# A hybrid conformer, mLSTM and mixture-of-experts block on one core: the last sigmoid products laid among the recurrence, SiLU rests and key products moved, one output-projection tile pair split into two passes, bias vectors loaded earlier

## The reference, cut to what matters

```python
u = rms_norm(h, norm_mix_g[l]);  z = u @ w_in[l] + b_in[l]          # h: 16 meta tokens + 512 tokens, 1024 wide
conv_out  = conformer_conv(z[..., GLU_OFF:Q_OFF], ...)              # GLU, 31-tap conv, layer norm, silu, pointwise matmul
mlstm_out = mlstm_branch(z, mlstm_norm_g[l], mlstm_out_w[l])        # recurrence, norm of each head, sigmoid gate, matmul
g_conv, g_mlstm = sigmoid(z[..., GC_OFF:GM_OFF]), sigmoid(z[..., GM_OFF:N_IN])
h = h + (g_conv * conv_out + g_mlstm * mlstm_out) @ w_out[l]
h = h + moe_ffn(rms_norm(h, norm_ffn_g[l]), ...)                    # 32 experts, top 4
out = rms_norm(h, final_norm_g)
```

## Time and profile before

| | us |
|---|---|
| median of 3 runs | 1623.09 (1620.73 to 1624.62) |
| time of the profiled execution | 1621.82 |
| its span | 1620.0 |
| PE busy | 1580.6 (98%) |
| GpSimd busy | 427.9 (26%) |
| DVE busy | 651.3 (40%) |
| ACT busy | 395.8 (24%) |
| chain that ended last: PE / DMA | 82% / 8% |

### The profile page before, as it was taken

How to read it: one execution, slowest core, us unless ns; L and a number is a source line. 1 busy time by engine, 2 the same in 40 slices (tenths; PEclk the granted TensorE clock), 3 DMA queues, 4 the chain that set the end, 5 groups by cost and what they waited for, 6 DMA issues and landing times.

```text
span 1620.0 us, 38897 instructions
## 1 busy us (share of the span) xinstructions
PE 1580.6 (98%) x16450; PEld 925.2 (57%) x16450; DVE 651.3 (40%) x1245; ACT 395.8 (24%) x605; POOL 427.9 (26%) x465
## 2 busy tenths in 40 slices
PE   6999999998999899999999999999999999999997
PEld 6998988876889634444444444334433444444444
DVE  4799898026241624222422242224222422242247
ACT  5333134255221511111111111111111111111112
POOL 7334334371433621211121112111211121112114
PEclk9999999999999899999999999999999999999999
DMA  7553243320275289999999999999999999999995
GB/s 215 157 182 105 79 144 90 105 78 27 78 298 212 84 300 411 408 409 414 413 408 403 410 411 406 406 409 410 399 409 406 411 395 402 407 411 400 400 416 243
DMA packets 132436, 492.91 MB, mean 304 GB/s; under 512 B 17305, under 2 KB 74817, under 8 KB 82628
## 3 DMA queue, kind: packets, MB, share of 16 engines
q1 hardware_dynamic: 114020, 464.98, 73.2%
q0 software_dynamic: 8736, 16.22, 3.1%
q10 hardware_dynamic: 9632, 11.03, 2.2%
HBM read 476.32 MB, written 24.87 MB: 309 GB/s over the span
## 4 chain that ended last, share of the span: by engine, by line
PE 82%; DMA 8%; POOL 2%; ACT 2%; DVE 2%; SPq 2%; issue 1%; POOLq 0%; DVEq 0%; ACTq 0%
PE banks L1532 36%; PE banks L1104 25%; PE banks L1581 17%; DMA w_ring<-in_expert_w_dram 7%; PE banks L1519 1%; POOL slot_table L693 1%; DVE mix_lo L1898 1%; SPq L442 1%; DMA small<-in_b_in_dram 0%; POOL h_res L759 0%; ACT banks L991 0%; ACT w_hi L800 0%; PE banks L1552 0%; ACT conv L954 0%; SPq L524 0%
## 5 line engine op out<-in xcount | busy, mean ns | idle before, releaser
L1532 PE MATMUL banks<-w_ring,xT 128*32 128x512 f32 x6144 | 671.5, 592 | 4.9 <-DMA w_ring<-in_expert_w_dram 4.0
L1532 PEld LDWEIGHTS banks<-w_ring,xT 128*32 128x32 f32 x6144 | 206.9, 110 | 429.9 <-issue 423.6
L1581 PE MATMUL banks<-w_ring,actT 128*32 128x256 f32 x6144 | 344.6, 380 | 0.0
L1581 PEld LDWEIGHTS banks<-w_ring,actT 128*32 128x32 f32 x6144 | 205.7, 110 | 134.3 <-issue 18.0
L2011 DVE TENSOR_TENSOR hid<-banks,bias 128x512 f32<-128x512 f32 x96 | 63.9, 665 | 477.4 <-PE banks L1532 477.4
L633 POOL TENSOR_TENSOR w_lo<-stage,w_hi 128x2048 fp32r<-128x2048 f32 x38 | 175.2, 4611 | 264.1 <-ACT w_hi L800 264.1
L1104 PE MATMUL banks<-u_hi,w_hi 128*128 128x264 f32 (+1 forms) x528 | 175.6, 333 | 0.3 <-ACT gates L914 0.3
L1104 PE MATMUL banks<-u_hi,w_lo 128*128 128x264 f32 (+1 forms) x528 | 174.6, 331 | 0.0
L1104 PE MATMUL banks<-u_lo,w_hi 128*128 128x264 f32 (+1 forms) x528 | 174.2, 330 | 0.0
L703 POOL COPY token_now<-token_of 96x1 int32 (+1 forms) x33 | 6.1, 183 | 568.7 <-PE banks L1519 564.9
L1065 ACT ACTIVATE bias<-banks 128x512 f32<-128x512 f32 x32 | 19.1, 597 | 560.5 <-PE banks L1552 560.5
(11 more groups left out here) (298 smaller groups left out, 1626.8 us busy)
## 6 DMA issues: line engine op xcount, KB each, us to landing
w_ring<-in_expert_w_dram SPq DMA_DIRECT2D x384, 1024.0 KB, 22.5
stage<-in_w_in_dram SPq DMA_DIRECT2D x20, 1024.0 KB, 5.3
stage<-in_w_in_dram SPq DMA_DIRECT2D x16, 512.0 KB, 5.3
y_rows<-empty_row ACTq DMA_DIRECT2D x8, 1024.0 KB, 4.7
y_in<-y_rows SPq DMA_DIRECT2D x4, 2048.0 KB, 22.4
stage<-in_conv_pw_w_dram SPq DMA_DIRECT2D x4, 1024.0 KB, 5.1
stage<-in_mlstm_out_w_dram SPq DMA_DIRECT2D x4, 1024.0 KB, 5.1
stage<-in_w_out_dram SPq DMA_DIRECT2D x4, 1024.0 KB, 5.5
```

The lines of the kernel that those rows point to most:

```text
L1532: last = nc.tensor.matmul(banks[32 * g:32 * (g + 1), t].rearrange("p (c j) -> p c j", j=64), xT[:, k, 32 * t:32 * (t + 1)], units, start=k ...
L1581: last = nc.tensor.matmul(banks[32 * g:32 * (g + 1), 3 + t, 0:GRP], actT[:, t, k], w2_ring[k // 2][:, k % 2, GRP * g:GRP * (g + 1)], start ...
```

## The change

Six edits in one. (1) The four tiles of the last sigmoid pair are taken apart (`last_sigmoid`): two stand before the meta-token state products, the third before the state products of chunk 1, the fourth behind the numerators of tile 0, with two state products and the key transposes of chunk 2 inside it after its fifth k-step. The third and fourth go into bank 0, not banks 4 and 5. (2) The squares go to a bf16 scratch in SBUF (`head_squares`, over `mean_w`) and not to PSUM, and the numerators of the next tile wait on `h_taken`, not on `h_squared`. (3) The key transposes of chunk 3 stand inside the numerators of tile 2; `pointwise(0, 0)` is cut in two, its first tile ahead of the hidden transposes of tile 2. (4) On DVE `silu_rests(0)` leaves its place before tile 0 and stands with `silu_rests(1)` behind tile 1; on ACT the order of sigmoids, splits, keys and `silu_highs` follows; on GpSimd the second half of the PW weights is split behind the root of tile 0. (5) WO pair 0, half s=1: for token tiles 0 and 1 the products with `w_hi` run first, behind a wait for `w_hi` alone, and those with `w_lo` after `wait_weights`. (6) The second half of the first GLU pair is loaded behind the twelve vector transfers.

```diff
@@ sync
-            load_glu(0, first=True)
+            load_glu(0, (0,), first=True)
...
+            load_glu(0, (1,), first=True)
             sp.dma_start(vb_bc, b_in[:, V_OFF:V_OFF + D].to_broadcast([P, D])).then_inc(row_bc_in, 16)
@@ gpsimd
-            split_pair(PW_PAIR)
+            split_pair(PW_PAIR, (0,))
 
             for i in range(TT):
                 pool.wait_ge(h_squared, HEADS * (i + 1))
                 rstd(P, head_square, head_rstd, DV)
                 nc.gpsimd.tensor_tensor(head_scale, head_rstd, den_inv, ALU.mult).then_inc(h_scaled, 1)
+                if i == 0:
+                    split_pair(PW_PAIR, (1,))
@@ scalar
+            def head_sums(i):
+
                 act.wait_ge(h_taken, i + 1)
                 for h in range(HEADS):
-                    nc.scalar.activation(banks[:, 4 + h, 0:DV], h_buf[i % 2][:, h], ACT.Square, scale=den_inv[:, h:h + 1],
+                    if i or h >= 2:
+                        act.wait_ge(h_squared, HEADS * i + h - 1)
+                    nc.scalar.activation(head_squares[:, h % 2], h_buf[i % 2][:, h], ACT.Square, scale=den_inv[:, h:h + 1],
                                          accum_out=head_square[:, h:h + 1]).then_inc(h_squared, 1)
...
+            def last_sigmoid(t):
+
+                act.wait_ge(mm_done, pair_tick(SIG_PAIR + 5, LAST_TICKS[t]))
+                nc.scalar.activation(gates[:, 3 * KT - 4 + t], banks[:, LAST_BANKS[t]], ACT.Sigmoid,
+                                     bias=vec[:, B_SIG + 3 * KT - 4 + t:B_SIG + 3 * KT - 3 + t]).then_inc(sig_out, 1)
+
+            scaled_keys(0)
+            last_sigmoid(0)
+            last_sigmoid(1)
+            split_hi(PW_PAIR, 0)
+            scaled_keys(1)
+            last_sigmoid(2)
+            head_sums(0)
+            scaled_heads(0)
+            scaled_keys(2)
+            last_sigmoid(3)
+            split_hi(PW_PAIR, 1)
+            silu_highs(0)
+            for i in range(1, TT):
+                if i == 2:
+                    scaled_keys(3)
+                head_sums(i)
+                silu_highs(i)
+                scaled_heads(i)
+                split_hidden(i - 1)
             split_hidden(TT - 1)
@@ tensor
-            sigmoid_tiles(5)
...
+            def numerators(i):
+
                 pe.wait_ge(head_out, HEADS + 1)
-                pe.wait_ge(h_squared, HEADS * i)
+                if i:
+
+                    pe.wait_ge(h_taken, i)
                 for h in range(HEADS):
                     nc.tensor.matmul(banks[:, 4 + h, 0:VW], probs[:, h, P * i:P * (i + 1)], v_sb[:, i, h], start=True, stop=False)
                     pe.wait_ge(state_out, HEADS * i + h + 1)
                     nc.tensor.matmul(banks[:, 4 + h, 0:VW], q_sb[:, h, P * i:P * (i + 1)], state[:, h],
                                      start=False, stop=True).then_inc(h_mm, 1)
+                    if i == 2 and h == 2:
+                        key_transposes(3)
+
+            def rest_of_state():
+                state_part(1, (2, 3))
+                key_transposes(2)
+
+            wait_weights(SIG_PAIR + 5, 0)
+            pe.wait_ge(sig_out, 3 * KT - 5)
+            last_sigmoid(0)
+            pe.wait_ge(sig_out, 3 * KT - 4)
+            last_sigmoid(1)
+            state_part(0)
+            key_transposes(1)
+            wait_weights(SIG_PAIR + 5, 1)
+
+            pe.wait_ge(normed, KT)
+            last_sigmoid(2)
+            state_part(1, (0, 1))
+
+            pe.wait_ge(sig_out, 3 * KT - 2)
+            numerators(0)
+            pe.wait_ge(sig_out, 3 * KT - 1)
+            last_sigmoid(3, rest_of_state)
+            for i in range(1, TT):
+                numerators(i)
+                if i + 1 < TT:
                     hidden_transposes(i - 1, (0,))
                     state_part(i + 1, (0, 1))
                     hidden_transposes(i - 1, (1,))
                     state_part(i + 1, (2, 3))
                 else:
-                    hidden_transposes(i - 1)
-
                     pe.wait_ge(state_out, HEADS * TT)
                     pe.wait_ge(silu_lo_made, KT)
-                    pointwise(0, 0)
+                    pointwise(0, 0, (0,))
+                    hidden_transposes(i - 1)
+                    pointwise(0, 0, (1,))
             hidden_transposes(TT - 1)
...
+                    if j == 0:
+                        pe.wait_ge(w_hi_made[1], WO_PAIR + 1)
+                        for low in range(2):
+                            if low:
+                                wait_weights(WO_PAIR, 1)
+                            for i in range(2):
+                                span = slice(P * i, P * (i + 1))
+                                for k in range(KT):
+                                    terms = ((mix_hi, w_lo),) if low else ((mix_hi, w_hi), (mix_lo, w_hi))
...
+                    for i in range(0 if j else 2, TT):
@@ vector
             update_state(0)
-            silu_rests(0)
             for i in range(TT):
...
+                if i == 1:
+                    silu_rests(0)
+                    silu_rests(1)
+                elif i == 2:
+                    silu_rests(2)
                 if i >= 2:
                     split_rest(i - 2)
-                if i:
-                    silu_rests(i)
```

More of the change, by code:

```diff
@@ L1338, in _, with pointwise @@
             whole = slice(0, SEQ)
-            def pointwise(j, s):
+            def pointwise(j, s, parts=range(GT)):
                 wait_weights(PW_PAIR + j, s)
-                for c in range(GT):
+                for c in parts:
                     if j:
@@ L1425, in _ @@
                         continue
-                    for i in range(TT):
+                    if j == 0:
[7 more added lines that the diff above has]
+                                    terms = ((mix_hi, w_lo),) if low else ((mix_hi, w_hi), (mix_lo, w_hi))
+                                    for m, (rows, w) in enumerate(terms):
+                                        last = nc.tensor.matmul(banks[:, 4 + i, GRP:2 * GRP], rows[:, k, span], w[:, 1, k],
+                                                                start=not low and k == 0 and m == 0, stop=low == 1 and k == KT - 1)
+                                if low:
+                                    last.then_inc(mm_done, 1)
+                    for i in range(0 if j else 2, TT):
                         token_tile(s, (mix_hi, mix_lo), banks[:, 4 * (1 - j) + i, GRP * s:GRP * (s + 1)],
```

44 lines of the change are left out of this document (16 added, 28 removed).

## The result

| | before | after |
|---|---|---|
| median | 1622.74 us (1620.73 to 1624.62, 4 runs) | 1609.63 us (1607.62 to 1610.73, 4 runs) |
| profiled execution | 1621.82 | 1610.73 |
| its span | 1620.0 | 1609.0 |

Two longer comparisons later gave the same program 0.9931 (0.9917 to 0.9946) and 0.9938 (0.9924 to 0.9951), 11.2 and 10.1 us; all 15 runs of it have a median of 1610.7. So some 2 to 3 us of the 13.1 were the draw of these runs, and 4 to 5 us are left for which the prediction must answer.

What follows compares the result with a forecast made beforehand. PE was taken to bound everything before the experts. Recurrence 4.0 (9.6 - 3.9 - 1.7), WO 1.9 and start 0.5 sum to 6.4 us: profiled 1621.8 becomes 1615.4, median 1.3 above, 1616.7 us; range 1612.3 to 1621.3.

Steps and rivals of the forecast that it cites:

- the 1.82: PE's hole at 24.5, waiting for the vectors: removed there but probably moved to the third GLU unit; 0.5 us taken as won.
- Its landing times: At the start, the second GLU half lands at 26.2 and is ready for PE at 33.0, wanted at 31.0.
- their terms: New PE holes in the recurrence: 0.7 for DVE's state, 2.0 for tok_made, 0.9 for chunk 3 keys, 0.3 for silu_lo; 3.9 us.
- I count one slow stretch: In the recurrence's new order, one half-clock stretch near the new hole at 377 costs 1.7 us; bounds none and two.
- both slow stretches lose their cause: Recurrence, 360 to 366 and 370 to 376: meta products between dense tiles and no hole at 367 remove causes of 3.4 us.
- rival C: Recurrence: DVE's rests meet GpSimd's w_lo, delaying DVE and tile 1's root 4 us; recurrence wins nothing, 1620.7 us; chance 0.20.
- WO: Output projection: PE's 1.90 us hole at 495.8 goes whole, 1.9 us won, at least 1.5 for an added handoff.
- D: Experts: their stream, at DMA share 1.01, starts by something other than PE, hiding the gain; 1623 us; chance 0.06.
- B: Recurrence and start: no slow stretch (1.7) and the vectors' 1.8 won whole, 3.0 us more, 1613.7 us; chance 0.20.
- the 1.8: At the start, the vectors' stall is won whole if small transfers hold the queue for less than 5.2 us.
- no slow stretch at all: Recurrence: between dense tiles the rows show no cause for a lower clock, so 1.7 us more is won.
- E: Start: second GLU half issued only after small transfers leave the queue; PE loses 8.0 us there, 1625.2 us; chance 0.04.

Runs made afterwards that it cites:

- the moved root: Changed kernel with the second half of the PW weights split behind the root of tile 1 on GpSimd, not ahead of it: 1614.99 us, ratio 0.9954.
- the PSUM run: Changed kernel with edit 2 undone, squares written back to PSUM and the next numerators waiting on them: one profile, 1610.43 us.
- the fills: Changed kernel with unread products before the third GLU unit and tile 1's hidden transposes: 1616.01 us oversized, with router fills too; 1617.74 us resized, without them.
- WO alone: Kernel before with only the output projection's edit (5): 1619.35 us, ratio 0.9988.
- vectors alone: Kernel before with only the new order of the first loads (edit 6): 1618.39 us, ratio 0.9985.
- the start filled: Kernel before with 16 unread products laid where PE waits for the vectors at 24.5: 1620.30 us against 1622.18, ratio 0.9988.
- The recurrence alone: Kernel before with only the edits of the recurrence (1 to 4): 1615.67 us, ratio 0.9966.

## Why the prediction was right and wrong

Since single profiles differ by the stretches, I take for each part the mean over the profiles whose order and holes are the same in that part (their count in brackets).

| stretch | old order | new order | won | forecast |
|---|---|---|---|---|
| start to key transposes | 336.6 (4) | 333.7 (7) | 3.0 | 0.5 |
| to `pointwise(0, 1)` | 70.6 (5) | 66.1 (5) | 4.5 | 4.0 |
| to the router, at full clock | 129.4 (4) | 127.2 (9) | 2.2 | 1.9 |
| router to the end | 1082.2 (5) | 1082.6 (5) | -0.4 | 0 |

Sum 9.2, where the runs say 10 to 11; the 1 to 2 us between stand in no row. (The second row leaves out the moved root, the PSUM run and the fills; the fourth takes, for the new order, the changed kernel's three profiles, the PSUM one and the moved root, and leaves out WO alone for the old, which would make the -0.4 a -0.3.)

**The start: wrong, and the step that failed is the price of the hole.** The prediction costed "the 1.82" as idle time and asked only whether it moves. Its landing times were right to 0.2 us. But the hole also brings a slow stretch behind it, 2.1 us in the mean of four profiles, and the moved hole doesn't; with 0.9 that the hole itself is shorter by (2.05 us at 24.5 in the mean of four profiles, 1.11 at 31 in the mean of seven), that makes 3.0 where I took 0.5. That is 2.5 of the 4 to 5 us that were to be explained. In the profile of before nothing showed it, since that execution happened to have none at 26; the same profile did show it at 360 and 370, and there I had priced it. I priced the clock where the one profile had it, and not where the same kind of hole stood without.

**The recurrence: right in the mean, for half of the reasons.** Each hole went where the rows said, and the new ones came within 0.3 us of their terms (0.7, 2.0, 0.9, 0.3 forecast; 0.66, 2.07, 0.63, 0.16 found). Wrong is the step "I count one slow stretch": the old order loses 2.05 us of work in the mean of five profiles, the new one 2.05 too (none twice, 3.4 three times). So "both slow stretches lose their cause" was wrong: with the meta products between dense tiles their stretch came in five of nine profiles, and behind the new hole at 377 there was one in five of seven. The change won nothing by the clock here.

Wrong too, though it didn't show in the sum, is that each stretch of the old order costs its 1.7. Where it lies on the first numerators (before in both profiles, and WO alone), the hole behind it is 2.20; where it comes only behind that hole (vectors alone, and the start filled), the hole is 3.90. Vectors alone:

```profile
367.61 1.72 PE L1336 MATMUL banks<-v_sb,kw_sb 128*128 128x257 f32 x4 [3.90 <-DVE state L1829]
```

PE stands there for DVE, which comes at the same time either way, so the slow numerators were covered by the wait. And DVE is late through its three rests, which in the profile of before (as in the other four) stand beside a `w_lo` until 365.02:

```profile
360.50 4.52 POOL L633 TENSOR_TENSOR w_lo<-stage,w_hi 128x2048 fp32r<-128x2048 f32 x1 [2.50 <-ACT w_hi L800]
```
```profile
362.55 4.22 DVE L1851 TENSOR_TENSOR silu_lo<-conv,silu_hi 128x512 fp32r<-128x512 f32 x3 [1.85 <-ACT silu_hi L982]
```

Three rests without `w_lo` take 1.89. So rival C's meeting already stood in the kernel before, under the name of DVE's state update, and edit 4 takes `silu_rests(0)` out of it; what that edit is worth alone no run shows.

At the full clock the old order would take 69.85 us (WO alone and the second profile of before, whose only stretch is a covered one), the new one takes 64.57: 5.3 won, 4.3 of it idle time. From this 0.8 goes off in the mean, because slow stretches make the new order 1.6 us longer and the old one, with one of its places covered, only 0.8. That gives the 4.5 of the table (in idle time 6.73 less 3.48, in busy time 63.90 less 62.66). Why the busy rows are 1.0 to 1.2 us shorter for the same matmuls I can't name. The first profile, with no slow stretch, shows 6.96; the 2.5 above the mean are luck in both profiles of that pair, before with one stretch that cost and after with none.

**WO: right.** 2.16 in every pair of profiles at full clock, against 1.9. The 0.3 more is not shown. The recurrence alone, which keeps this hole, had a slow stretch behind it once (494 to 500); the other four that keep it, none.

**The router: left out.** Its slow stretches lose 1.7 to 5.1 us of PE's work in all profiles without a fill. Leaving them out did no harm, because the chain to the second expert runs through GpSimd's slot table, SP and the weights, and not through them. Of the 1.5 us in the first table 1.3 are GpSimd's: from the router's first product until GpSimd was through with its last indirect transfer it was 32.27 us before and 31.01 after, but 31.00 in the second profile of before, and 31.27 with the moved root, whose router stage loses the same 5.1 us as before. They are no part of the change.

**Of the rivals**, C fell for this kernel, while its mechanism and its 4.3 us are shown by the root that was moved. D (hidden by the expert stream) is wrong for the 9 us ahead of the router, since GpSimd's first slot-table transfer follows PE there; for PE's time within the router stage something like it holds. B came nearest, 1613.7, by a larger term for the start, though not by its reason (the 1.8 did not go whole, the hole moved); its other term, no slow stretch at all, was true of one profile in three. E did not occur: the half landed 10.3 us after its issue, not 11 after a later one.

**The range** ended 1.6 (all 15 runs) to 2.7 us (the four) too high: it took the hole's length for the most that the start could bring. With the 2.1 of the clock at the start the sum would have been 8.5, the forecast 1614.6 and the low end 1610.2: the 1610.7 of all 15 runs would lie inside, the 1609.63 of the first four still below.

## What to carry to other kernels

A hole in PE between dense stretches has two prices, its length and the half clock that may follow, and one profile shows only one draw of the second: where one such hole has a slow stretch behind it, cost the chance of one at its fellows too, and look at a second profile before you call a place clean. A slow stretch ahead of a wait for another engine costs nothing as long as the wait covers it; compare the wait with and without it. And where a wait names DVE, look whether DVE itself stood for GpSimd. Before moving an operation of GpSimd to free a wait, ask which two-input operations of DVE it will now run beside; here a gain of 1.8 us cost 4.3 one step on. A gain counts only as far as the next stage that starts by something else: follow the chain there before you fill PE's waits.

## What the runs showed of the hardware that I had not expected

- An idle time of 1.8 to 2.4 us was followed by 1.7 or 3.4 us lost at the half clock in three of four executions; 2.1 us of useless products in its place made the kernel faster by 1.9. What decides whether a stretch comes in a given execution is open, as is why the hole of 0.5 to 1.6 us at 31 never brought one, in seven profiles.
- The slow stretches lose 1.7 us or a multiple of it (3.4, 5.1), in every stage. On the first numerators of the old order such a 1.7 cost nothing: the hole behind was 2.20 with it and 3.90 without.
- `w_lo` on GpSimd, which began at 375.93 while DVE's second rest was running, was itself 0.4 longer (4.97 against 4.55); the third rest, which began behind it, took 5.02 in place of 0.68. A GpSimd operation on 4 columns takes 0.68 beside a two-input operation of DVE and 0.21 without; the power behind it 1.34 and 1.06.
- The remainder of a run, from the router on, moves by 4 us between executions of kernels that are equal there (1080.6 to 1084.6): nearly as much as the largest part of this change brings.
